# Block sums of the channel mixer's weights: down sums by accumulating DMAs during attention, up sums and sums of x on VectorE, stores of combinations on GpSimd's queue

## The reference

```python
h = rmsnorm(x);  z = h @ w_in                       # 1024 x 3120, columns shared out among three mixers
o = concat(gla(z), sparse_attention(z), mlstm(z))   # 256 + 512 + 256
x = x + o @ w_out
x = x + relu(rmsnorm(x) @ w_up) ** 2 @ w_down       # 1024 x 4096 and 4096 x 1024
```

## Time and profile before

| what | us |
|---|---|
| three runs | 1925.2, 1925.57, 1929.59 (median 1925.57) |
| profiled execution | 1918.35, of it the span of the trace 1916.6 |
| busy in the span | PE 1694.0, DVE 1091.9, ACT 736.7, POOL 261.9 |

### The profile page before, as it was taken

How to read it: one execution, slowest core, us unless ns; L and a number is a source line. 1 busy time by engine, 2 the same in 40 slices (tenths; PEclk the granted TensorE clock), 3 DMA queues, 4 the chain that set the end, 5 groups by cost and what they waited for, 6 DMA issues and landing times. The chain is left out here.

```text
span 1916.6 us, 34635 instructions
## 1 busy us (share of the span) xinstructions
PE 1694.0 (88%) x13909; PEld 1558.6 (81%) x13909; DVE 1091.9 (57%) x1814; ACT 736.7 (38%) x1379; POOL 261.9 (14%) x276
## 2 busy tenths in 40 slices
PE   7725998678799999799999779779999989999998
PEld 6625997678688888678876369779999989999998
DVE  6305326521278777556667775876666675545542
ACT  6311223110166555544445432343333343333331
POOL 1101000000122222332221132410000000000000
PEclk9866998798889999899999789989999999999999
DMA  7998889999941001357749756236556578665652
GB/s 171 151 300 202 154 165 283 283 225 204 226 100 24 2 2 44 117 202 244 235 148 271 167 171 196 75 117 218 175 186 189 182 247 285 184 200 185 196 174 62
DMA packets 339037, 333.61 MB, mean 174 GB/s; under 512 B 62190, under 2 KB 272710, under 8 KB 336254
## 3 DMA queue, kind: packets, MB, share of 16 engines
q1 hardware_dynamic: 309102, 226.20, 41.4%
q0 software_dynamic: 27392, 100.67, 20.0%
q10 hardware_dynamic: 2384, 4.53, 0.7%
HBM read 261.50 MB, written 141.15 MB: 210 GB/s over the span
## 5 line engine op out<-in xcount | busy, mean ns | idle before, releaser
L59 PE MATMUL pm<-ops,slots 128*128 128x258 f32 x1792 | 511.1, 285 | 26.6 <-DVE ops L3694 19.5
L60 PE MATMUL pm<-ops,slots 128*128 128x258 f32 x1792 | 509.4, 284 | 0.0
L61 PE MATMUL pm<-ops,slots 128*128 128x258 f32 x1792 | 508.3, 284 | 0.0
L59 PEld LDWEIGHTS pm<-ops,slots 128*128 128x128 f32 x1792 | 340.6, 190 | 27.6 <-DVE ops L3694 20.2
L61 PEld LDWEIGHTS pm<-ops,slots 128*128 128x128 f32 x1792 | 342.9, 191 | 0.0
L60 PEld LDWEIGHTS pm<-ops,slots 128*128 128x128 f32 x1792 | 342.8, 191 | 0.0
L59 PE MATMUL pz<-hH,winH 128*128 128x344 f32 x600 | 209.9, 350 | 60.7 <-DVE zb L910 59.0
L3521 ACT ACTIVATE slots<-uact 128x512 fp32r<-128x512 f32 x224 | 137.4, 626 | 172.7 <-DMA uact<-upS_scratch 48.0
L60 PE MATMUL pz<-hL,winH 128*128 128x344 f32 x600 | 201.8, 336 | 0.0
L61 PE MATMUL pz<-hH,winL 128*128 128x344 f32 x600 | 201.0, 335 | 0.0
L3700 DVE TENSOR_TENSOR slots<-uact,slots 128x512 fp32r<-128x512 f32 x224 | 156.5, 708 | 75.5 <-ACT slots L3521 75.4
(11 more groups left out here) (671 smaller groups left out, 3232.5 us busy)
## 6 DMA issues: line engine op xcount, KB each, us to landing
hidD_scratch<-onat SPq DMA_DIRECT2D x112, 258.0 KB, 3.8
upS_scratch<-in_w_up_dram POOLq DMA_DIRECT2D x12, 2048.0 KB, 21.5
downS_scratch<-in_w_down_dram POOLq DMA_DIRECT2D x12, 2048.0 KB, 17.1
hs<-hidD_scratch SPq DMA_DIRECT2D x38, 516.0 KB, 4.8
uact<-upS_scratch SPq DMA_DIRECT2D x64, 256.0 KB
uact<-downS_scratch SPq DMA_DIRECT2D x64, 256.0 KB
raw<-in_w_in_dram SPq DMA_DIRECT2D x24, 512.0 KB, 14.9
uact<-in_w_up_dram SPq DMA_DIRECT2D x48, 256.0 KB
```

The lines of the kernel that those rows point to most:

```text
L59: nc.tensor.matmul(out, wH, mH, start=start and k == 0, stop=False)
L60: nc.tensor.matmul(out, wH, mL, start=False, stop=False)
L61: last = nc.tensor.matmul(out, wL, mH, start=False, stop=stop and k == n - 1)
```

## The change

- POOL no longer makes any block sum during project. `upS` is gone.
- The four down sums are made by the same 16 DMAs of 2 MB in attention. Eight copies and four accumulating DMAs are issued ahead of the first `scale_sliding`, two accumulating ones in front of the 29th window step and two in front of the 43rd.
- For each pair the mixer loads the four blocks of `w_up` once (4 x 256 KB instead of 7), and DVE makes the four up sums (`add_up`, 128 x 512, 64 in all).
- The four sums of x, twice, are made by DVE instead of POOL.
- The first seven units are split in v = 5 to 9 of the output projection instead of 10 to 15.
- The stores of combinations and the loads of x for the last sums (`store_form`, `load_acc`) are issued by POOL instead of SP.

```diff
 # project_and_prepare, gpsimd: the whole loop over which (begin, add, slot) is removed
-                for which in range(2):
...
-                    slot(1)
-                    begin(0, block_of(1, 0))
...
-                    for n in range(2):
-                        slot(11 + n)
-                        add(3, n, sums[2, :, :])
 # attend_prompt, gpsimd
+                def copy_sum(f, block):
+                    for n in range(2):
+                        rows = slice(n * D, (n + 1) * D)
+                        nc.gpsimd.dma_start(io["downS"][f, rows, :], block[rows, :], max_dma_last_dim=2048).then_inc(sums_done[f], 16)
+
+                def add_sum(f, block):
+                    pool.wait_ge(sums_done[f], 32)
+                    for n in range(2):
+                        rows = slice(n * D, (n + 1) * D)
+                        nc.gpsimd.dma_start(io["downS"][f, rows, :], block[rows, :], accum_op=ALU.add, max_dma_last_dim=2048).then_inc(sums_done[f], 16)
...
+                copy_sum(0, down_quarter(1, 0))
+                copy_sum(2, down_quarter(0, 0))
+                copy_sum(1, down_quarter(0, 0))
+                copy_sum(3, down_quarter(0, 1))
+                add_sum(0, down_quarter(1, 1))
+                add_sum(1, down_quarter(1, 0))
+                sliding = [s for s in range(len(sched.steps)) if sched.steps[s][1] == WIN]
                 for s in range(len(sched.steps)):
+                    if s == sliding[len(sliding) // 2]:
+                        pool.wait_ge(sums_done[0], 64)
+                        add_sum(2, io["downS"][0])
+                    if s == sliding[3 * len(sliding) // 4]:
+                        pool.wait_ge(sums_done[2], 64)
+                        add_sum(3, io["downS"][2])
 # mix_and_mixer, sync
+                def load_block(p, b):
+                    if p:
+                        if b < 3:
+                            sp.wait_ge(s_ready, 4 * (p - 1) + (4 if b == 1 else 3))
+                        if b != 2:
+                            sp.wait_ge(wL_ready, 7 * (p - 1) + (1, 3 if p > 1 else 2, 0, 6 if p > 1 else 5)[b])
+                    sp.dma_start(raw[b].rearrange("p (k n) -> p k n", k=4), up_block(p, b)).then_inc(w_in[b], 16)
...
+                for p in range(1, NPAIR):
+                    sp.wait_ge(used, 7 * p + 1)
+                    if p + 1 < NPAIR:
+                        for b in (0, 2, 1):
+                            load_block(p + 1, b)
+                        load_block(p + 1, 3)
 # mix_and_mixer, gpsimd: x_first to x_fourth removed, store_form and load_acc come from SP
+                for p in range(NPAIR):
+                    for f in (0, 2, 6, 4, 3, 1, 5):
+                        store_form(p, f)
 # mix_and_mixer, tensor: the first product
-                    pe.wait_ge(wL_ready, j + 1)
+                    if j == 0:
+                        pe.wait_ge(wL_ready, 7)
 # mix_and_mixer, vector
+                def add_up(p, f):
...
+                    for b in {4: (2, 3), 3: (0, 2), 1: (0,), 6: (1,)}[f]:
+                        dve.wait_ge(w_in[b], 16 * (p + 1))
+                    if f in (1, 6):
+                        nc.vector.drain()
+                    one, two = {4: (raw[2], raw[3]), 3: (raw[0], raw[2]), 1: (raw[0], sum_of(p, 4)), 6: (raw[1], sum_of(p, 1))}[f]
+                    nc.vector.tensor_tensor(sum_of(p, f), one, two, ALU.add).then_inc(s_ready, 1)
+
+                def x_first(c):
+                    nc.vector.drain()
+                    nc.vector.tensor_tensor(T1x, x_block(c, 0, 1), x_block(c, 0, 0), ALU.subtract).then_inc(xt_ready, 1)
...
+                    if v in (5, 6, 7):
+                        low_w(FIRST_ORDER[v - 5])
...
+                        if j == 3:
+                            add_up(p + 1, 4)
+                            add_up(p + 1, 1)
+                        if j == 4:
+                            add_up(p + 1, 3)
+                        if j == 5:
+                            add_up(p + 1, 6)
```

More of the change, by code:

```diff
@@ L3027, in mix_and_mixer @@
     w_down = io["w_down"].rearrange("l (j k p) n -> l j p k n", p=P, j=2)[0]
-    up_sums, down_sums = (io[n].rearrange("f (k p) n -> f p k n", p=P) for n in ("upS", "downS"))
+    down_sums = io["downS"].rearrange("f (k p) n -> f p k n", p=P)
     xT = io["xT"].rearrange("(k p) t -> p k t", p=P)
@@ L3061, in mix_and_mixer @@
         uact_flat = uact[:, :, :].rearrange("p a t -> p (a t)")
-        raw = [uact_flat[:, 512 * n:512 * (n + 1)] for n in range(3)]
+        raw = [uact_flat[:, 512 * n:512 * (n + 1)] for n in range(4)]
+        first_sums, later_sums = (hsf[:, D:D + 512], hsf[:, D + 512:D + 1024], hsf[:, D + 512:D + 1024]), (wo0[:, 0:512], wo0[:, 512:1024], unit[15][:, 0:512])
         ynat = [uact_flat[:, 1536:2048], unit[15][:, 0:512]]
@@ L3114, in free_room, with up_block, down_block @@
                     eng.wait_ge(evD, evicted(last))
[L3116 to L3120, removed]
-                second = slice(NPAIR * P + cols.start, NPAIR * P + cols.stop)
-                return w_up[int(f != 0), :, :, second if f == 5 else cols]
+        def up_block(p, b):
+            i, j = b // 2, b % 2
+            return w_up[j, :, :, (i * NPAIR + p) * P:(i * NPAIR + p + 1) * P]
+        def down_block(n):
             f, m, at = (n - NUP) // 16, (n - NUP) // 4 % 4, slice(n % 4 * 4, n % 4 * 4 + 4)
@@ L3219, in _ @@
                 for v in range(13, 16):
                     keep_x(v)
+                for b in (0, 2, 1, 3):
+                    load_block(1, b)
                 for n in range(4):
[L3222 to L3245 removed]
@@ new lines, in _ @@
+                    sp.wait_ge(late_sums[n], 64)
+                for p in range(1, NPAIR):
[4 more added lines that the diff above has]
+                        load_block(p + 1, 3)
+                for n in range(2):
+                    load_piece(n)
+                for n in range(NUP, NUP + 3):
+                    load_weights(n)
+                load_piece(2)
@@ L3590, in _ @@
                         high_x(0, 6)
-                    if v == 15:
-                        for n in range(5, 7):
-                            high_w(n)
                 square(15)
@@ L3853, in _ @@
                 scale_x(1, 3)
+                x_first(1)
                 for k in range(4, 8):
                     scale_x(1, k)
-                for o in range(6):
+                low_x(1, 0)
+                x_third(1)
+                low_x(1, 1)
+                x_second(1)
+                low_x(1, 2)
+                x_fourth(1)
+                for o in range(3, 6):
                     low_x(1, o)
@@ L3917, in program @@
     io["hidD"] = scratch("hidD", [P, 7, NPAIR, TT // 2])
-    io["upS"], io["downS"] = scratch("upS", [4, D // 2, 2 * D]), scratch("downS", [4, 2 * D, D // 2])
+    io["downS"] = scratch("downS", [4, 2 * D, D // 2])
     with ExitStack() as ctx:
@@ L3941, in program @@
             keep["late_z"] = nc.alloc_semaphore("late_z_stored")
-            keep["weight_sums"] = [[nc.alloc_semaphore(f"sums_{which}{n}") for n in range(4)] for which in ("up", "down")]
+            keep["weight_sums"] = [nc.alloc_semaphore(f"down_sums{n}") for n in range(4)]
             project_and_prepare(nc, io, keep)
```

218 lines of the change are left out of this document (105 added, 113 removed).

## The result

| | before | after | ratio |
|---|---|---|---|
| median of the first pair (4 and 4 runs) | 1925.38 us | 1827.07 us | 0.9489 [0.946, 0.9518] |
| second pair, another chip (9 and 5 runs) | 1917.64 us | 1825.06 us | 0.952 [0.95, 0.9539] |
| profiled execution of the first pair | 1918.35 us | 1834.37 us | |

The change is worth 93 to 98 us.

A forecast was written before the change was run, and what follows sets the result against it. It took project to wait on DMA engines filled by the block sums' traffic. Project -99, attention +57 and mixer -5 gave -47 us: 1871 us for the profiled execution, 1878 us for the median, range 1838 to 1912.

The forecast's parts named there:

- project's 81 us: Project after the stall: 81 us of waits and half clock, 25 left for DVE and stores, 56 us to come back.
- rival C: Project: PE's pace throughout, -124 us there, 1854 us in total; chance 0.12.
- Rival A: Project does not follow the DMAs: DVE's chain and SP's stores hold slots 11 to 18; only 68 back, 1910; chance 0.18.
- The stall: Project, PE's wait before slot 5: the whole 43.1 us goes, counted as 43 of the 99 us.
- Attention, +57: Attention: POOL's wait for copies delays the first window step by 54 us, later issues add 3; +57 us.
- 26.5 us of all engines for q and keys: Attention: its own loads, 80.2% of 33 us, added to 40 us for six copies in the delay.
- The even share: Attention: the two queues share the engines evenly, copies and loads both done by 73 us; delay 54 us.
- Rival B: Attention: POOL's wait is short, copies ahead of the loads, 29 us; total 1854 us; chance 0.14.
- strict order of issue: Attention: copies have the engines to themselves ahead of the loads, making the delay 29 us instead of 54.
- Mixer, -5: Mixer: tiles 9 to 15 -6 us, the second half's chain +1, pairs hidden under PE; -5 us, bounds -10 to +5.
- Rival D: Mixer pairs: the stores' issues on POOL block DVE, 25.0 against 20.0 us a pair, +75, total 1953; chance 0.06.
- Rival E: No net change: project gives back only 68 us and attention's delay is 64; total 1920 us; chance 0.05.

The follow-up runs named there:

- Run 1: The kernel before with none of the 32 DMAs that make block sums, the mixer loading plain blocks instead: 1793.66 us, ratio 0.9318 to the kernel before.
- run 7: The kernel before, up sums still in project, but down sums in attention with accumulating DMAs inside the step loop: 1864.98 us, ratio 0.9727 to the kernel before.
- runs 10 and 11: On one chip: first the kernel after unchanged, 1825.06 us; second the kernel after with early accumulating DMAs moved before the 15th window step, 1784.53 us.
- run 3: The kernel after with the accumulating DMAs of sums 0 and 1 issued before the 15th window step, not the first: 1789.84 us, ratio 0.9305 to before.
- run 6: The kernel after with copies in the order of sums 0, 1, 2, 3 in place of 0, 2, 1, 3: 1824.36 us, ratio 0.9526 to before.
- runs 1 and 2: First: the kernel before without any block-sum DMAs, 1793.66 us. Second: the kernel after without the 16 down-sum DMAs, plain blocks loaded instead, 1786.42 us.
- run 8: The kernel after with the stores of combinations on SP's queue instead of POOL's: 1824.23 us, ratio 0.9522 to the kernel before.
- Run 5: The kernel after with down sums in project, one copy behind each of slots 5 to 12, accumulating DMAs behind 13 to 23: 1810.52 us, ratio 0.945 to before.
- run 9: The kernel after with the four early accumulating DMAs replaced by plain copies to a second place, without waits: 1781.32 us, ratio 0.9298 to the kernel before.

## Why the prediction was wrong

The direction was right, and so were the mechanisms in outline; the forecast was 51 us off because two terms were mis-sized on the same side (28 us in project, 10 in attention) and the profiles' own scatter added to them.

**The step that failed: project's 81 us, "I leave 25 us".** I had split what lay between the slot-5 stall and the barrier into 283 us of work and 81 us of waits and half clock, and then kept 25 of the 81 for DVE's 12.2 us a slot, queued stores and two 2 MB stores. The profile after has 280 us from 110 to the barrier, the 283 of work and nothing more; `pz` waits 1.6 us in all. Run 1 shows that taking the sums' DMAs away is enough for it. What I held for the engines' own load went with the DMAs. Of PE's idle time before, 44.3 us did not stand in front of `pz` but in the work around the slots, and were put down to ACT and DVE (us in total, times, longest; 153 to 517 us):

```profile
PE pn L427 <- ACT hold L685: 19.7, 4, 8.1
PE pl L452 <- ACT hold L713: 9.1, 2, 7.6
PE pl L442 <- DVE cbias L1049: 8.0, 1, 8.0
PE pn L417 <- DVE zb L984: 7.5, 2, 4.5
```

They look like engines at their limit, but in after such waits come to 2.0 us (1.0 + 0.6 + 0.4), and in run 1 to 3.4. And with DVE's work denser than before (0.65 of the time between 200 and 250 us) PE is busy 49.0 of 50 us. The term measured -127.1 (-122.6 in run 1), rival C's -124. My chance for C, 0.12, was too low: ACT's idle time was put down to `raw`, and I had written that down as the argument against A without drawing the second half of it. How the traffic reached the waits around the slots was not traced further. Rival A is refuted.

**The stall.** -43 was right: no stall at 110, and run 7 shows that the up sums alone bring it (48 us).

**Attention, +57.** Measured +47.0 in that profile, 40.5 by the medians of runs 10 and 11 (the place in run 3 costs 1 to 3.4 us at most). The mechanism holds: the 5th and 6th copies, then `add_sum(1)`, then the first scaling. The term that was mis-sized is the loads. I had added 26.5 us of all engines for q and keys beside the 40 of six copies. From the first copy's issue to POOL's release it took 59.8 us, where I had 71 (75 - 4). The queues in this stretch:

```profile
q0 software_dynamic: 3849, 15.32, 75.9%
q1 hardware_dynamic: 2479, 5.34, 25.5%
```

That is 45.4 us for the copies (40 for six, the rest for a part of the others) and 15.2 for the loads. So the loads took 15.2 us of the 26.5. A part of those is q blocks that SP loads only once PE has used the ones before, and PE stood still: SP's next load of q is issued at 459.08 us. The issues in the loop took 2.6 us a pair in front of two steps; the waits there found their semaphores, as predicted. The even share was not what failed. The Trainium skill, "DMA: Bandwidth & Descriptors", section "Queues, rings and completion order", has each DMA engine go round its queues packet by packet; the trace agrees to one packet in 600. Since a packet of the copies carries twice the bytes, the copies had 69% while both queues had work, not 50%. That did not move the sum: by 440 us the loads were done (2.5% of the engines' time from 430 to 440), well ahead of the sixth copy, and it paid for all of them either way. Rival B (29 us) is refuted by the delay of 45.5, and strict order of issue by the equal packets. What I had not seen at all is the queue's room of run 6: with it, an earlier semaphore would not have helped.

**Mixer, -5.** -3.3 between the first profiles, -8.6 between runs 1 and 2 and -7.2 by their medians: right within what can be told. Over all profiles the mixer of before takes 804.0 to 810.0 us (before, runs 1 and 7), that of after 797.6 to 801.5. The parts: tiles 9 to 15 take 37.5 us, -7.2 (I had 38 to 39, -6). From tile 15 to PE's last wait in the second half it is 27.6 us after 29.1 (1172.38 - 1144.74, 1258.56 - 1229.41), -1.5 where I had +1: the waits there are 7.76 + 5.60 us after 6.43 + 7.66. Together that is 8.7 us. The first pair shows only 3.3 because after is 3.1 us slower ahead of tile 9 (75.2 us after 72.0) and 2.3 behind the last wait. Ahead of tile 9 that is scatter: run 10, the same kernel, has 72.2, and run 1, with the mixer of before, 74.7.

**Rival D** is refuted: PE stays full in the pairs with DVE at 0.78, and run 8 without POOL's issues is not faster. DVE beside such an issue, in after:

```profile
1399.53 0.69 DVE L3670 TENSOR_TENSOR slots<-uact,slots 128x512 fp32r<-128x512 f32 x1
1402.53 0.69 DVE L3670 TENSOR_TENSOR slots<-wo,slots 128x512 fp32r<-128x512 f32 x1
```

```profile
1402.91 1.07 POOL L3270 DMA_DIRECT2D hidD_scratch<-onat  x2 [4.60 <-DVE onat L3739]
```

The second `slots` overlaps the issues and takes the 0.69 us of the first; an issue is 0.54 us, not 1.3. Rival E did not come either.

**The rest.** By the profiles the change was worth 84 us, by medians 98 and 93. The first two profiles lay 7 us to either side of their medians. I had allowed for the 7 of before, which are in the forecast; the 51 us are 37 by the stages and 14 by these two distances, and no term of mine could have had the 14.

## What to carry to other kernels

Look at the DMA share beside a load loop: at 0.95 and above the loads landed in 11.8 to 14.9 us and PE waited, at 0.68 they landed in 3.7. Run 5 moved the same bytes at half the price by spreading them. The price of each kind (6.6 and 12.3 us of all engines per 2 MB) says how many fit under one step.

When a load loop's idle rows name one resource, forecast that the next engine's pace is reached, unless that engine's own busy time forbids it. Waits put down to side work may go with the same resource, as 42 of PE's 44.3 us did here.

And issue background transfers that wait for others where their semaphores have long fired and those others have left the queue. Four accumulating DMAs ahead of the first step of an in-order queue cost 41 us; the same DMAs in front of the 15th step cost 1 to 3.4. An earlier semaphore alone (run 6) gained nothing.

## What the runs showed of the hardware

- Two queues with work on the same 16 engines shared them packet for packet (600 and 601 in 10 us, 611 and 610 in the next 10), not by bytes or time: 69.3% and 33.5% of the engines' time for packets of 4 and 2 KB.
- In run 6 a fourth accumulating DMA of 2 MB left POOL 10.95 us late with nothing to wait for, with three accumulating ones and first four, then three copies under way. It left 0.4 us after the sixth copy landed, when two were. Twelve copies (run 9) left at once, and so did four accumulating DMAs in run 3, with at most two copies under way. The accumulating ones seem to take more of some room in the queue than copies do. Which room was not tried.
- While the DMA share stood at 1.0 and more, PE's matmuls in attention ran on: between 453 and 500 us PE is busy 42.4 of 47 us with q0 at 103%.
- PE's granted clock was 0.50 (1.2 GHz) from 410 to 460 us of after, in which PE was busy 3.1 us, 0.68 in the next 10 us, with PE full, and 1.00 (2.4 GHz) in the 10 after them.
